# Hybrid decoder step on one core: inverse roots of the recurrence heads' norm by Ln and Exp on ScalarE instead of Sqrt and a VectorE reciprocal

## What is computed

```python
def rmsnorm(x, g):
    y = xf * lax.rsqrt(jnp.mean(xf * xf, axis=-1, keepdims=True) + EPS)
    return (y * g)
...
o_a = rmsnorm(o_a, g_attn_out)
...
o_h = rmsnorm(o_h, g_hg_out) * jax.nn.silu(g_h)
x = x + gt1 * (concatenate([o_a, o_h]) @ w_out)
h = rmsnorm(x, g_ffn) * (1.0 + sc2) + sh2
x = x + gt2 * moe_ffn(h, ...)
```

## Time and profile before

| what | value |
|---|---|
| median of three runs | 1177.12 us (1176.06 to 1179.9) |
| the profiled execution's own time | 1177.35 us |
| its span, first to last instruction | 1175.6 us |
| TensorE busy (matmul) | 1099.1 us, 93% of the span |
| VectorE busy | 345.2 us, 29% |
| ScalarE busy | 162.9 us, 14% |
| GpSimd busy | 55.8 us, 5% |
| DMA | 461.65 MB, mean 393 GB/s |
| mean granted TensorE clock | 0.997 |

### The profile page before, as it was taken

How to read it: one execution, slowest core, us unless ns; L and a number is a source line. 1 busy time by engine, 2 the same in 40 slices (tenths; PEclk the granted TensorE clock), 3 DMA queues, 4 the chain that set the end, 5 groups by cost and what they waited for, 6 DMA issues and landing times.

```text
span 1175.6 us, 14105 instructions
## 1 busy us (share of the span) xinstructions
PE 1099.1 (93%) x5497; PEld 440.7 (37%) x5497; DVE 345.2 (29%) x761; ACT 162.9 (14%) x313; POOL 55.8 (5%) x86
## 2 busy tenths in 40 slices
PE   7999999999999999989898989898989898989896
PEld 3677756633333333233222323232323232322222
DVE  4154377431322213222222222222222212221214
ACT  3232171301010001000100010001000100000003
POOL 1140002010000000000000000000000000000000
PEclk9999999999999999999999999999999999999999
DMA  9881299999999999999999999999999999999994
GB/s 366 323 290 72 90 388 378 351 351 417 430 430 429 431 430 430 430 432 430 430 429 431 431 430 431 430 430 430 430 432 429 431 431 430 431 430 429 430 429 203
DMA packets 49128, 461.65 MB, mean 393 GB/s; under 512 B 6657, under 2 KB 7873, under 8 KB 22202
## 3 DMA queue, kind: packets, MB, share of 16 engines
q1 hardware_dynamic: 42512, 445.17, 90.7%
q0 software_dynamic: 5600, 13.13, 3.1%
q10 hardware_dynamic: 986, 2.95, 0.7%
HBM read 460.30 MB, written 5.78 MB: 396 GB/s over the span
## 4 chain that ended last, share of the span: by engine, by line
PE 57%; DMA 38%; DVE 3%; issue 1%; ACT 0%; SPq 0%; ACTq 0%; DVEq 0%
PE bank L1599 27%; DMA arena<-in_w_up 17%; DMA ring<-in_w_up 17%; PE bank L1479 6%; PE bank L1623 4%; DMA arena<-in_w_down 3%; PE bank L896 2%; PE bank L1392 2%; PE bank L1062 2%; PE bank L1592 2%; PE bank L1148 1%; PE bank L1011 1%; PE bank L1041 1%; PE bank L994 1%; PE bank L1132 1%; PE bank L1485 1%
## 5 line engine op out<-in xcount | busy, mean ns | idle before, releaser
L1599 PE MATMUL bank<-arena 128*64 128x512 f32 x1024 | 239.9, 600 | 12.1 <-DMA arena<-in_w_up 11.5
L1599 PE MATMUL bank<-ring,arena 128*64 128x512 f32 x1024 | 240.0, 601 | 9.7 <-DMA ring<-in_w_up 8.5
L1599 PEld LDWEIGHTS bank<-arena 128*64 128x64 f32 x1024 | 67.3, 136 | 165.1 <-issue 149.5
L1599 PEld LDWEIGHTS bank<-ring,arena 128*64 128x64 f32 x1024 | 66.0, 136 | 163.4 <-issue 137.6
L1623 PE MATMUL bank<-arena 128*64 128x512 f32 x512 | 114.6, 596 | 9.0 <-DMA arena<-in_w_down 9.0
L1623 PE MATMUL bank<-ring,arena 128*64 128x512 f32 x512 | 114.6, 596 | 8.9 <-DMA ring<-in_w_down 8.9
L2167 DVE TENSOR_SCALAR arena<-bank 128x256 f32<-128x256 f32 x64 | 24.1, 419 | 274.7 <-PE bank L1599 274.7
L1479 PE MATMUL bank<-arena,mods 128*128 128x512 f32 (+1 forms) x204 | 93.7, 630 | 0.9 <-DVE arena L2194 0.9
L850 ACT ACTIVATE arena<-arena 128x512 f32<-128x512 f32 x32 | 20.2, 630 | 493.0 <-DVE arena L2167 493.0
L2156 DVE TENSOR_TENSOR x<-x,bank 128x512 f32<-128x512 f32 x64 | 44.0, 687 | 144.5 <-PE bank L1479 144.5
L896 PE MATMUL bank<-const,arena 128*128 128x128 f32 (+3 forms) x348 | 51.1, 286 | 21.3 <-DMA ring<-in_w_down 7.6
(11 more groups left out here) (336 smaller groups left out, 802.0 us busy)
## 6 DMA issues: line engine op xcount, KB each, us to landing
ring<-in_w_up SPq DMA_DIRECT2D x64, 2048.0 KB, 34.1
arena<-in_w_up SPq DMA_DIRECT2D x64, 2048.0 KB, 34.3
ring<-in_w_down SPq DMA_DIRECT2D x32, 2048.0 KB, 33.7
arena<-in_w_down SPq DMA_DIRECT2D x31, 2048.0 KB, 33.4
ring<-in_w_ada SPq DMA_DIRECT2D x16, 1024.0 KB, 12.5
ring<-in_w_ada SPq DMA_DIRECT2D x16, 512.0 KB, 10.8
ring<-in_w_in SPq DMA_DIRECT2D x3, 2048.0 KB, 15.0
ring<-in_w_in SPq DMA_DIRECT2D x5, 1024.0 KB, 12.8
```

The costliest lines, as they stand in the source:

```text
L1599: mm = pe.matmul(B[2 * e + c % 2][64 * a:64 * a + 64, :], lhsT=xTe[:, k, 64 * e:64 * e + 64], rhs=big(PER * s + n)[:, r, 512 * c:512 * (c ...
```

## The change

The two roots of the recurrence heads leave the helper. ScalarE takes Ln of the mean plus eps from the bank into `r_hg[t]` and gives the bank back; then, for both halves, waits for its own Ln, and takes Exp of -0.5 times the value in place, which is the inverse root. A new semaphore `powers` counts the Exp. VectorE waits for `powers` instead of the bank, its reciprocal is gone, and the product stays. The other roots of the stretch (as1, as0, hsd, asd) stay Sqrt with a reciprocal.

```diff
@@ -761,7 +761,11 @@
                 copy_probs(i)
             take_values(1)
             for t in range(2):
-                root(r_hg[t], f"hs{t}", heads(f"hs{t}"), P)
+                wait_filled(act, f"hs{t}")
+                act.activation(r_hg[t], heads(f"hs{t}"), ACT.Ln, scale=1.0 / P, bias=eps).then_inc(emptied(f"hs{t}"), 1)
+            for t in range(2):
+                wait_emptied(act, f"hs{t}")
+                act.activation(r_hg[t], r_hg[t], ACT.Exp, scale=-0.5).then_inc(sem("powers"), 1)
             take_values(0)
             wait_emptied(act, "ada2")
@@ -1934,8 +1938,7 @@
             def norm_heads(t):
-                wait_emptied(dve, f"hs{t}")
-                link(dve.reciprocal(r_hg[t], r_hg[t]))
+                dve.wait_ge(sem("powers"), t + 1)
                 wait_emptied(dve, f"hgo{t}")
                 part = cat[:, 4:8, P * t:P * (t + 1)]
                 dve.tensor_tensor(part, part, r_hg[t], ALU.mult).then_inc(sem("hg_ready"), 1)
```

## The result

Sixteen runs of each kernel gave a median of 1180.46 us (1178.09 to 1183.64) after and 1177.55 us (1176.06 to 1179.9) before: a ratio of 1.0023, 95% interval 1.0013 to 1.0032, slower by 2.7 us (1.5 to 3.8). Forecast were 1178.6 us and +1.5 us. A second set of runs of the unaltered changed kernel, further down, gave 1.0022 (1.0013 to 1.0032), so the 2.7 us are real.

A forecast was written before the change was run, and what follows sets the result against it. TensorE's arrival at the experts, which starts the weight stream, was taken to bound the kernel. A 1.81 us wait less 0.31 us gave +1.5 us on the 1177.12 us median: 1178.6 us, range 1176.3 to 1180.4.

The forecast's parts named there:

- Bound and path: Whole run: a microsecond TensorE gains or loses before the expert weight stream starts at 245 us comes out at the end.
- The reciprocals on the chain are worth 0.31 to 0.65 us: VectorE's L1938: removing 6.7 us of reciprocals gives TensorE only 0.31 us, plus at most 0.34 us at 190.66 us.
- Three table loads, two Exp: ScalarE from 167.40 us: loads for Ln, Exp and as1's Sqrt, two more than before at 1.28 us; Exp pair 1.15 us.
- single load for ln and exp: Rival, ScalarE's table loads: Ln and Exp share a set, one load fewer, 1177.3 us; chance 0.07.
- drain that the Trainium skill puts beside each load: Rival, ScalarE: each added load costs twice its row; 1181.2 us, or 1181.4 by the skill's 1.38 us drain; chance 0.03.
- TensorE's wait of 1.81 us, net 1.5: TensorE ahead of dpv (L1342): waits for as1's bank 1.81 us, less the old 0.31 us; projection starts at 187.96 us.
- The term left at zero in the forecast's sum: TensorE's clock: the +1.5 us sum included nothing for a fall, which was priced only as a rival at 1.7 us.
- The prediction's sign against itself: TensorE: a clock below 1.00 between 176 and 190 us was listed among the signs that the forecast was wrong.
- the likeliest case: Whole run: the summed forecast of 1178.6 us, own range 1177.8 to 1179.6, given chance 0.67.
- the clock's rival: TensorE behind the new stall at 174.74 us: the clock falls, 1.7 us more, 3.2 in all, 1180.3 us; chance 0.09.

The follow-up runs named there:

- e4_no_recip: Kernel before without the two VectorE reciprocals of L1938 and nothing in their place, so heads are multiplied by the root itself; ratio 0.9984 (0.9974 to 0.9994).
- e8_late_exp: Against the kernel before: Ln for hs0, hs1, as1, as0 behind one load, all Exp after as0's, four reciprocals gone, VectorE steps reordered; 0.9997 (0.9987 to 1.0007).
- e3_act_only: Kernel before, Sqrt and reciprocals kept, plus two Exp of 128x512 on a scratch tile after the two Sqrt, bringing two more loads; ratio 1.0009 (0.9998 to 1.0020).
- after_p1: The changed kernel unaltered, run once more for a further profile; 1181.7 us.
- e2_banks: Changed kernel with dpv and dT exchanging banks and as0's root moved ahead of the od0 and od1 copies; ratio to the kernel before 0.9999 (0.9989 to 1.0008).
- e7_before_again: The kernel before, unaltered, run again for a second profile; ratio 0.9997 (0.9987 to 1.0006).
- before_p1: The kernel before, unaltered, run once more for a further profile; 1176.94 us.
- e5_fill2: Changed kernel with two extra 128x512 TensorE products ahead of dpv, filling the 1.8 us wait; ratio to the kernel before 1.0027 (1.0015 to 1.0038).

## Why the prediction was right, and where it was short

*Bound and path.* Right: what TensorE loses ahead of the experts comes out at the end. The time from the first expert product to the end is 933.2 to 934.5 us in thirteen of the fourteen profiles (936.0 in the other), with 75.5 to 82.5 us ahead of it.

*The reciprocals on the chain are worth 0.31 to 0.65 us.* Right by the profiles: 0.4 us in e4_no_recip and e8_late_exp, and nothing behind a late ScalarE (e3_act_only). The runs of e4_no_recip gave 1.9 (0.7 to 3.1), which this and their higher clock explain in part.

*Three table loads, two Exp.* Right to 0.04 us: as1's Sqrt was put at 176.13, which with this execution's 0.59 us is 176.72, and came at 176.68. The Trainium skill's single load for ln and exp ("ScalarE: Activation LUTs", "Table sets: the hidden batching unit") was not what happened here: L765 and L768 each have a load. The drain that the Trainium skill puts beside each load (the same page, "What ACT_TABLE_LOAD costs") doesn't show either: Ln starts 1.29 us after its load does, and Exp's load 0.02 us after the Ln pair's end.

*TensorE's wait of 1.81 us, net 1.5.* Right: 1.80 us, and 22.39 us from the head squares to the projection in the one profile without a fall there (after_p1), where 22.41 had been forecast (187.96 - 165.55). e2_banks, which takes away this wait and leaves the loads and both Exp, brings the time back.

*The step that fell short: the clock.* The prediction read one profile of the kernel before, whose clock falls at 232 us, and priced a fall as a rival that the new idle time might bring, 1.7 us with a chance of 0.09. The size was right (1.6), the cause and the chance were not. The clock falls ahead of the projection without any wait too (e7_before_again, before_p1, e2_banks, e4_no_recip, e8_late_exp), and filling the wait doesn't prevent it (e5_fill2). The term left at zero in the forecast's sum is the 1.2 us between 1.5 and 2.7, and the runs' clock puts about one fall more per execution in its place (1.7 us of clock). Time and clock come back when the delay goes (e2_banks: 0.9999, clock 0.9962), and neither does when the delay is filled with work (e5_fill2: 1.0027, clock 0.9950). The Trainium skill, "TensorE: Matmul & The Clock Gate", section 'Part 1: The HAM clock gate (the "warmup" mystery)', says that the monitor behind the clock runs freely and does not start anew with a kernel; that the same kernel has its fall at 180 in two profiles and at 232 to 233 in two others agrees with that. Why a fall more goes with a delay of 1.8 us, and not with one of 7 us, is not settled by these runs. The prediction's sign against itself, a clock below 1.00 between 176 and 190 us, came true but tells nothing, as the kernel before shows it too; and the falls, with the 0.59 us from ahead of the change, put the projection at 191.68 and the first reload at 249.02 us, where 188.0 and 246.9 had been named.

*Range and verdict.* The ratio, on the 1177.12 us from which the forecast was made, is 1179.8 us: inside the range of 1176.3 to 1180.4, and just outside the likeliest case's own 1177.8 to 1179.6. That the range held it is in part luck: it had been widened to 1180.4 for the clock's rival, whose cause was wrong. The move of 0.23% is below the 0.3% that had been taken for what a measurement can tell, though with sixteen runs of each kernel the interval excludes no change.

## What to carry to other kernels

A reciprocal on the chain of waits is worth what the bounding engine idles for it, here 0.31 us of 6.7; read that engine's own timeline for gaps before pricing a removal. Work added to an engine that looks 14% busy is priced by which PSUM banks it gives back late and who needs them next: the same three loads and two Exp cost nothing that the runs could tell once two bank names were exchanged and one root moved up, nor did three loads and four Exp with the Exp behind the last bank. Where a stretch has a fall of the clock now and then, one profile shows one draw of it; take several before calling the stretch clean.

## What the runs showed of the hardware that was not expected

The granted clock falls in stretches in which TensorE's records show it busy all the time (0.50 from 179 to 189 us in e2_banks, with at most 0.4 us idle ahead of it). A fall loses 1.70 or 1.71 us of clock in these profiles, and the long one of e2_banks three times that; its place differs between executions of one kernel. How much clock is lost differs too, and is part of why the times spread over 4 to 6 us: in the three sets of runs of the kernel before, the 14 with a mean clock of 0.994 took 1179.3 us in the mean, the 39 with 0.997 1177.1.
